# Second attention: the rotation's swapped halves brought by transfers from ScalarE's queue, not by products; query and key blocks in two banks

## The chip, the core and the metric

One core of a Trainium2 chip runs the kernel, with its engines TensorE (PE in the profile), VectorE (DVE), ScalarE (ACT), GpSimd (POOL) and SyncE (SP), the last of which only issues transfers. The metric is the time of one execution on the device in microseconds, the median of several runs.

## What is computed

The reference is a first block (a gated recurrence and a sparse attention side by side, then a feed-forward), and two further layers on the same 256 tokens of 1024 features, each an attention and a convolutional feed-forward. The change is in the attention of the first of the two further layers, called the second attention here:

```python
def apply_rope(x, cos, sin):
    half = x.shape[-1] // 2
    x1, x2 = x[..., :half], x[..., half:]
    ...
    return jnp.concatenate([x1 * c - x2 * s, x2 * c + x1 * s], axis=-1)

def moba_mixer(xn, w_qkv, w_o, cos, sin):
    ...
    q = apply_rope(qkv[:, :, 0], cos, sin)
    k = apply_rope(qkv[:, :, 1], cos, sin)
    o = moba_attention(q, k, qkv[:, :, 2])
    return o.reshape(B, S, N_HEADS_2 * HEAD_DIM) @ w_o
```

With 256 tokens there is one block, so the attention is a causal one over 16 heads of 64 features. The rotation takes each head's features in two halves of 32 and needs, beside x, the same x with its halves swapped and the second half negated.

## The kernel before

Features lie on the 128 partitions, tokens along the free dimension. All weights come from one stream of 356 chunks of 128 x 1024 numbers (512 KB), which SP loads in order into three raw buffers (L543). Every chunk is split into a high part by ScalarE (`split_high`, L1291) and a low part by VectorE (`split_low`, L1776), into rings of six, and every product of full accuracy is three products on TensorE: high with high, high with low, low with high (`split_product`, L610 to L612). The order on each engine is the order of the code; semaphores join the engines, and no scheduler decides anything.

The second attention has, after its values, 16 blocks of projections (`query_or_key`): even ones are queries, odd ones keys, each of two heads, 24 products from one chunk. Three of them come ahead, in banks 0, 1 and 2; the others all go to bank 3 and are placed by `next_queries_and_keys` between the parts of the attention, two per pair of heads j. So TensorE's order in a pair is: scores of the pair (L729), block 3 + 2j, turning of the probabilities of pair j - 2 (L741), block 4 + 2j, values of pair j - 3 (L756 to L759). The turning begins with the third pair, the values with the fourth; in the first two pairs two blocks follow each other directly.

Each block then goes through this:

- ScalarE copies it out of its bank to `rope_in` (L1637, two buffers), and goes on to the split of a chunk six ahead.
- TensorE multiplies `rope_in` by a constant matrix `rot64` of zeros, ones and minus ones into bank 7 (`turn_rope`, L1094), in the middle of the next block's products. In the trace this product is two instructions.
- VectorE (`rope`) multiplies `rope_in` by the cosines (L2216), bank 7 by the sines (L2218) and adds the two (L2219). It signals `rope_done`, for which the scores wait: pair j needs blocks 2j and 2j + 1.

ScalarE's order in a pair (`attention`, `behind_block`) is: output of pair j - 4 (L1367, from j = 4), two heads' exponentials (L1358, L1360), the copy of block 3 + 2j and a split, the copy of turned probabilities (L1374), the copy of block 4 + 2j and a split. VectorE's is: the low part of output j - 4 (L1800), two heads' row maxima (L1844, L1846), the inverse sums, block 2 + 2j, a copy of turned probabilities (L1859), block 3 + 2j. Each block on VectorE ends with a split. The code that sets where blocks go:

```python
        def qk_bank(n):
            return bank[min(n, QK_AHEAD)][:, 0:S]
...
            def rope_operand(n):
                act.wait_ge(chunk_used, BASE["qk1"] + n + 1)
                if n >= 2:
                    act.wait_ge(rope_done, n - 1)
                fn(rope_in[:, n % 2, :], qk_bank(n), ACT.Copy,
                   scale=1.0 if n % 2 else HD ** -0.5).then_inc(rope_in_ready, 1)
                split_high(BASE["qk1"] + n + RING)
```

## Time and profile before

| | |
|---|---|
| median of 3 runs | 1151.5 us (1149.93 to 1153.06) |
| the profiled execution | 1151.86 us |
| its span | 1150.1 us |
| TensorE busy | 1121.8 us, 98% |
| VectorE busy | 873.7 us, 76% |
| ScalarE busy | 689.9 us, 60% |
| chain that ended last | TensorE 82%, VectorE 7%, ScalarE 4%, transfers 3% |
| the stage of the change, first block to last scores | 572.3 to 641.1 us |

The busy time of an engine counts its arithmetic. Waiting, registers and the issuing of transfers are not in it. The start of an instruction is measured; the end of a product on TensorE is modelled, so that durations of neighbouring products overlap, and the distance of their starts is what one costs. Times of the chain and of rows count from the start of the span.

### The profile page before, as it was taken

The page shows a single profiled execution, that of the slowest core. Times are in us where ns is not written, and L with a number is a line of the kernel's source. Part 1 is how long each engine was busy: PE and PEld are TensorE (multiplying, and loading weights), DVE is VectorE, ACT ScalarE, POOL GpSimd, SP SyncE. Part 2 cuts the span into 40 slices and gives each one's busy share as a digit, 9 for nine tenths or more (in the row PEclk, how much of TensorE's full clock was granted, in tenths as well). Part 3 has the DMA queues.
Part 4 walks back from the last instruction along what each step waited for, and adds up shares of the span by engine and source line. Part 5 has one row for each costly group of instructions (what it writes and reads, how often), then busy time and mean ns, then how long its engine had stood idle before and what let it go on. Part 6 is the DMA issues. An engine that isn't in the chain of part 4 may idle for free.

```text
span 1150.1 us, 25241 instructions
## 1 busy us (share of the span) xinstructions
PE 1121.8 (98%) x9449; PEld 1086.1 (94%) x9449; DVE 873.7 (76%) x1640; ACT 689.9 (60%) x1240; POOL 89.6 (8%) x141
## 2 busy tenths in 40 slices
PE   6999999999999999999999999999999999999997
PEld 6999999988999999999899999999998889999997
DVE  5789878687587998888777578767677867877774
ACT  6757864566646666555665466555565846655554
POOL 0000000055300000000023200000001330000000
PEclk9998999999999999999999999999999999999999
DMA  6675644722274776665544247766653424776661
GB/s 224 202 217 158 201 140 130 215 80 83 62 205 142 207 225 200 192 197 185 165 147 128 82 153 223 215 193 195 187 153 121 129 76 150 225 213 196 190 195 38
DMA packets 52925, 190.89 MB, mean 166 GB/s; under 512 B 6000, under 2 KB 6256, under 8 KB 52848
## 3 DMA queue, kind: packets, MB, share of 16 engines
q1 hardware_dynamic: 52416, 188.64, 54.1%
q8 instruction: 53, 0.87, 0.3%
q10 hardware_dynamic: 432, 1.19, 0.3%
q14 instruction: 24, 0.20, 0.1%
HBM read 188.75 MB, written 1.05 MB: 165 GB/s over the span
## 4 chain that ended last, share of the span: by engine, by line
PE 82%; DVE 7%; ACT 4%; DMA 3%; issue 2%; SPq 0%; DVEq 0%; ACTq 0%
PE bank L610 24%; PE bank L611 23%; PE bank L612 23%; DMA w_raw<-weight_stream 3%; DVE w_low L1776 3%; PE bank L729 2%; PE bank L741 2%; ACT w_high L1291 1%; DVE arena L2015 1%; PE bank L618 1%; PE bank L620 1%; PE bank L619 1%; PE bank L758 1%; DVE r_low L1800 1%; PE bank L756 1%
## 5 line engine op out<-in xcount | busy, mean ns | idle before, releaser
L1776 DVE TENSOR_TENSOR w_low<-w_raw,w_high 128x1024 fp32r<-128x1024 f32 x356 | 433.8, 1223 | 137.1 <-ACT w_high L1291 134.1
L1291 ACT ACTIVATE w_high<-w_raw 128x1024 fp32r<-128x1024 f32 x356 | 374.9, 1059 | 263.3 <-PE bank L612 163.6
L610 PE MATMUL bank<-h_high,w_high 128*128 128x256 f32 x1760 | 498.4, 283 | 11.9 <-DVE h_low L1814 10.3
L611 PE MATMUL bank<-h_low,w_high 128*128 128x256 f32 x1760 | 488.8, 278 | 0.0
L612 PE MATMUL bank<-h_high,w_low 128*128 128x256 f32 x1760 | 488.7, 278 | 0.0
L610 PEld LDWEIGHTS bank<-h_high,w_high 128*128 128x128 f32 x1760 | 332.4, 189 | 17.3 <-issue 11.9
L611 PEld LDWEIGHTS bank<-h_low,w_high 128*128 128x128 f32 x1760 | 332.6, 189 | 0.4
L612 PEld LDWEIGHTS bank<-h_high,w_low 128*128 128x128 f32 x1760 | 332.3, 189 | 0.0
L610 PE MATMUL bank<-r_high,w_high 128*128 128x256 f32 x942 | 267.6, 284 | 4.7 <-ACT arena L1703 2.6
L611 PE MATMUL bank<-r_low,w_high 128*128 128x256 f32 x942 | 262.2, 278 | 0.0
L612 PE MATMUL bank<-r_high,w_low 128*128 128x256 f32 x942 | 262.2, 278 | 0.0
L610 PEld LDWEIGHTS bank<-r_high,w_high 128*128 128x128 f32 x942 | 178.4, 189 | 10.5 <-ACT arena L1703 4.7
L611 PEld LDWEIGHTS bank<-r_low,w_high 128*128 128x128 f32 x942 | 178.4, 189 | 0.3
L612 PEld LDWEIGHTS bank<-r_high,w_low 128*128 128x128 f32 x942 | 178.5, 189 | 0.0
L584 POOL TENSOR_SCALAR arena<-arena,stats 128x128 f32<-128x128 f32 (+1 forms) x128 | 82.4, 658 | 428.7 <-DVE stats L1853 428.6
L1893 DVE SCALAR_TENSOR_TENSOR arena<-arena,small 128x255 f32<-128x255 f32 (+1 forms) x184 | 87.8, 477 | 5.7 <-ACT arena L1407 2.4
L1800 DVE TENSOR_TENSOR r_low<-arena,r_high 128x256 fp32r<-128x256 f32 (+1 forms) x96 | 43.1, 450 | 7.1 <-ACT r_high L1420 4.0
L1407 ACT ACTIVATE arena<-arena,small 128x256 f32<-128x256 f32 x68 | 40.0, 588 | 13.2 <-DVE arena L1907 13.2
L1907 DVE TENSOR_TENSOR arena<-bank,rstd 128x256 f32<-128x256 f32 x68 | 28.8, 423 | 18.3 <-PE bank L612 18.2
L1358 ACT ACTIVATE arena<-bank,stats 128x128 f32<-128x128 f32 x64 | 23.3, 364 | 30.9 <-DVE stats L1846 30.9
L729 PE MATMUL bank<-arena 64*128 64x128 f32 (+3 forms) x256 | 34.4, 346 | 0.5 <-DVE arena L2295 0.3
L1420 ACT ACTIVATE r_high<-arena 128x256 fp32r<-128x256 f32 x68 | 27.8, 408 | 10.7 <-DVE arena L1931 9.6
(207 smaller groups left out, 1077.2 us busy)
## 6 DMA issues: line engine op xcount, KB each, us to landing
w_raw<-weight_stream SPq DMA_DIRECT2D x356, 512.0 KB, 4.1
x<-x_in SPq DMA_DIRECT2D x4, 256.0 KB, 6.2
small<-small_in ACTq DMA_DIRECT2D x1, 1001.5 KB, 9.1
out<-arena SPq DMA_DIRECT2D x3, 256.0 KB, 2.5
out<-arena SPq DMA_DIRECT2D x1, 128.0 KB, 2.7
out<-arena ACTq DMA_DIRECT2D x1, 128.0 KB, 2.9
small<-small_in ACTq DMA_DIRECT2D x1, 30.5 KB, 4.0
```

The lines of the kernel that those rows point to most:

```text
L584: ins = nc.gpsimd.tensor_scalar(part, part, inv_sums[:, t, h:h + 1], gate(i, t), ALU.mult, ALU.mult)
L610: mm(out_ap, wh, high, start=start, stop=False, skip_group_check=True)
L611: mm(out_ap, wh, low, start=False, stop=False, skip_group_check=True)
L612: return mm(out_ap, wl, high, start=False, stop=stop, skip_group_check=True)
L729: ins = mm(of(use.scores, i)[:, at], q(i, t)[part, :], k(i)[part, 0:P * (t + 1)], start=i not in seen, stop=i in seen, skip_group_check=True)
L1291: fn(w_high[:, c % RING, :], w_raw[:, c % RAW, :], ACT.Copy).then_inc(high_ready, 1)
L1407: fn(taps_g[:, j % 2, :], scaled_g[:, j % 2, :], ACT.Identity, scale=tap(f"fcw{n}", 2, k + j), bias=tap(f"fcb{n}", 0, k + j)).then_inc(tap ...
L1420: fn(r_high[:, j % SLOTS, :], hidden[:, j % 2, :], ACT.Copy).then_inc(hid_high, 1)
L1776: v.tensor_tensor(w_low[:, c % RING, :], w_raw[:, c % RAW, :], f(w_high[:, c % RING, :]), ALU.subtract).then_inc(low_ready, 1)
L1800: v.tensor_tensor(dst, src, f(high), ALU.subtract).then_inc(done, 1)
L1893: return v.scalar_tensor_tensor(dst[:, tokens:S], src[:, 0:S - tokens], tap(row, j), dst[:, tokens:S], ALU.mult, ALU.add)
L1907: v.tensor_tensor(scaled_g[:, slot, :], bank[slot][:, 0:S], rstd[:, :], ALU.mult).then_inc(g_scaled, 1)
```

## The change

- `qk_bank`: blocks from 3 on alternate between bank 3 (odd) and bank 7 (even). Block n waits for the copy of block n - 2, not of n - 1. Block 4 also waits until bank 7 has been read by the stage before, which the first rotation product did.
- `turn_rope`, its 16 products, the matrix `rot64` and the semaphore `rope_turned` are gone.
- ScalarE waits behind each copy for the copy's own semaphore and issues four transfers, each of 32 partitions x 256 numbers (32 KB), from `rope_in` to a new buffer `rope_swap`, so that the halves of both heads of the block are exchanged. The two buffers have a semaphore each. The split follows.
- VectorE's second product reads `rope_swap` and waits for the four transfers. The minus sign is now in the table of sines.
- The first scores also wait until their bank has been read (`rotated_and_bank`).

```diff
-         ("c64", S), ("s64", S), ("rot64", P), ("cs32", S),
+         ("c64", S), ("s64", S), ("cs32", S),
...
+        rope_swap = tiles(14336, 2)
...
-        rope_turned = sem("rope_turned")
+        rope_swapped = [sem(f"rope_halves_swapped{i}") for i in range(2)]
...
         def qk_bank(n):
-            return bank[min(n, QK_AHEAD)][:, 0:S]
+            return bank[n if n < QK_AHEAD else (QK_AHEAD, 7)[n % 2 == 0]][:, 0:S]
...
-            def turn_rope(n):
-
-                if n == 0:
-                    pe.wait_ge(acc_read, 4 * ACC_V1 + 4)
-                pe.wait_ge(rope_in_ready, n + 1)
-                if n:
-                    pe.wait_ge(rope_done, n)
-                mm(bank[7][:, 0:S], par("rot64"), rope_in[:, n % 2, :], start=True, stop=True).then_inc(rope_turned, 1)
-
             def query_or_key(n):
 
                 c = BASE["qk1"] + n
                 chunk_here(c)
-                if n > QK_AHEAD:
-                    pe.wait_ge(rope_in_ready, n)
+                if n == QK_AHEAD + 1:
+                    pe.wait_ge(acc_read, 4 * ACC_V1 + 4)
+                if n > QK_AHEAD + 1:
+                    pe.wait_ge(rope_in_ready, n - 1)
                 for k in range(DT):
                     ins = split_product(qk_bank(n), c, k * P, h_high[:, k, :], h_low[:, k, :], k == 0, k == DT - 1)
-                    if n and k == DT // 2 - 1:
-                        turn_rope(n - 1)
                 ins.then_inc(chunk_used, 1)
...
-                if (j, part) == (NH // 2 - 2, 1):
-                    turn_rope(SIZE["qk1"] - 1)
...
+            def rotated_and_bank(h):
+                pe.wait_ge(rope_done, 2 * (h // 2) + 2)
+                if h == 0:
+                    pe.wait_ge(acc_read, 4 * ACC_V1 + 3)
...
                 fn(rope_in[:, n % 2, :], qk_bank(n), ACT.Copy,
                    scale=1.0 if n % 2 else HD ** -0.5).then_inc(rope_in_ready, 1)
+                act.wait_ge(rope_in_ready, n + 1)
+                for at in range(0, P, HD // 2):
+                    other = at ^ HD // 2
+                    act.dma_start(rope_swap[at:at + HD // 2, n % 2, :], rope_in[other:other + HD // 2, n % 2, :]).then_inc(
+                        rope_swapped[n % 2], 16)
                 split_high(BASE["qk1"] + n + RING)
...
-                dve.wait_ge(rope_turned, n + 1)
-                link(v.tensor_tensor(b, bank[7][:, 0:S], s64r, ALU.mult))
+                dve.wait_ge(rope_swapped[n % 2], 64 * (n // 2 + 1))
+                link(v.tensor_tensor(b, rope_swap[:, n % 2, :], s64r, ALU.mult))
...
-    put("s64", np.sin(angles(HD)))
+    signs = np.where(row % HD < HD // 2, -1.0, 1.0).astype(np.float32)
+    put("s64", np.sin(angles(HD)) * signs[:, None])
```

ScalarE before, in the pair j = 4, behind the exponentials (L1637 is the copy, L1291 the split, L1374 the copy of turned probabilities, L1367 the next output).

```order
L1637 ACTIVATE arena<-bank3 128x256 [waits rope_done,chunk_used]
L1291 ACTIVATE w_high<-w_raw 128x1024 [waits chunk_used,chunk_loaded1]
L1374 ACTIVATE arena<-bank1 128x384 [waits pv_done,probs_turned]
L1637 ACTIVATE arena<-bank3 128x256 [waits rope_done,chunk_used]
L1291 ACTIVATE w_high<-w_raw 128x1024 [waits chunk_used,chunk_loaded2]
L1367 ACTIVATE r_high<-bank2 128x256 [waits pv_done]
```

The same place after the change (the copy is now L1632, the transfers L1637, the split L1286, the copy of turned probabilities L1369, the output L1362):

```order
L1632 ACTIVATE arena<-bank3 128x256 [waits rope_done,chunk_used]
L1637 DMA arena<-arena 32x256 [waits rope_operand_ready]
L1637 DMA arena<-arena 32x256 x3
L1286 ACTIVATE w_high<-w_raw 128x1024 [waits chunk_used,chunk_loaded1]
L1369 ACTIVATE arena<-bank1 128x384 [waits pv_done,probs_turned]
L1632 ACTIVATE arena<-bank7 128x256 [waits rope_done,chunk_used]
L1637 DMA arena<-arena 32x256 [waits rope_operand_ready]
L1637 DMA arena<-arena 32x256 x3
L1286 ACTIVATE w_high<-w_raw 128x1024 [waits chunk_used,chunk_loaded2]
L1362 ACTIVATE r_high<-bank2 128x256 [waits pv_done]
```

Eight transfers stand between copies and splits, and the second block is read from bank 7.

TensorE before, at the turn from one pair to the next (the end of a block of pair j = 1, the scores of pair 2, and the head of its first block up to the rotation product; left out are the products L611 and L612 and the L610 that only repeat):

```order
L1094 MATMUL bank7<-arena,small 128x256 [waits rope_done,rope_operand_ready]
L610 MATMUL bank3<-h_high,w_high 128x256
L729 MATMUL bank4<-arena 128x128 [waits rope_done,probs_ready]
L729 MATMUL bank5<-arena 128x256 [waits rope_done]
L729 MATMUL bank4<-arena 128x256
L729 MATMUL bank5<-arena 128x128
L610 MATMUL bank3<-h_high,w_high 128x256 [waits rope_operand_ready,low_ready]
```

The same place after the change:

```order
L611 MATMUL bank7<-h_high,w_high 128x256
L730 MATMUL bank4<-arena 128x128 [waits rope_done,probs_ready]
L730 MATMUL bank5<-arena 128x256 [waits rope_done]
L730 MATMUL bank4<-arena 128x256
L730 MATMUL bank5<-arena 128x128
L611 MATMUL bank3<-h_high,w_high 128x256 [waits rope_operand_ready,low_ready]
```

The rotation product is gone, and the scores still wait for `rope_done`.

## Rows read from the trace of the kernel before

**Rows 1.** The page: busy time of TensorE, and granted clock in 40 slices.
```profile
PE 1121.8 (98%) x9449; PEld 1086.1 (94%) x9449; DVE 873.7 (76%) x1640; ACT 689.9 (60%) x1240; POOL 89.6 (8%) x141
...
PEclk9998999999999999999999999999999999999999
```

**Rows 2.** Busy times by stretch, cut at starts of scores; then the stages behind.
```profile
core 0: us, PE busy (x) PEld busy (x) DVE busy (x) ACT busy (x) POOL busy (x), PEclk, DMA share, GB/s
581.34:589.65 8.31, 7.73 (x61) 7.17 (x60) 5.98 (x17) 5.55 (x13) 0.00 (x0) 1.00 0.59 183
...
615.27:624.36 9.09, 9.09 (x78) 8.34 (x76) 6.98 (x19) 5.03 (x15) 2.93 (x4) 1.00 0.41 116
...
633.46:641.10 7.64, 7.64 (x64) 6.95 (x62) 6.61 (x19) 4.34 (x13) 2.93 (x4) 1.00 0.39 112
657.00:1110.00 453.00, 445.99 (x3812) 437.23 (x3812) 342.53 (x583) 259.68 (x439) 24.36 (x36) 1.00 0.58 175
```

**Rows 3.** Timeline of TensorE around the first rotation product (start us, us, instruction).
```profile
576.02 0.28 PE L611 MATMUL bank<-h_low,w_high 128*128 128x256 f32 x1
576.14 0.28 PE L612 MATMUL bank<-h_high,w_low 128*128 128x256 f32 x1
576.25 0.59 PE L1094 MATMUL bank<-arena,small 128*128 128x256 f32 x2
576.50 0.47 PE L610 MATMUL bank<-h_high,w_high 128*128 128x256 f32 x1
576.80 0.28 PE L611 MATMUL bank<-h_low,w_high 128*128 128x256 f32 x1
```

**Rows 4.** Timeline of TensorE from block 3 to block 4.
```profile
585.37 0.28 PE L612 MATMUL bank<-h_high,w_low 128*128 128x256 f32 x1
586.23 0.36 PE L610 MATMUL bank<-h_high,w_high 128*128 128x256 f32 x1 [0.58 <-ACT arena L1637]
```

**Rows 5.** Timeline of ScalarE: copies of blocks 0 and 1.
```profile
575.60 0.40 ACT L1637 ACTIVATE arena<-bank 128x256 f32<-128x256 f32 x1
...
578.27 0.39 ACT L1637 ACTIVATE arena<-bank 128x256 f32<-128x256 f32 x1 [1.29 <-PE bank L612]
```

**Rows 6.** Timeline of ScalarE in the pair j = 4, in brackets what it waited.
```profile
615.79 0.38 ACT L1367 ACTIVATE r_high<-bank 128x256 fp32r<-128x256 f32 x1
617.30 0.37 ACT L1358 ACTIVATE arena<-bank,stats 128x128 f32<-128x128 f32 x1 [1.14 <-DVE stats L1846]
...
619.62 0.38 ACT L1637 ACTIVATE arena<-bank 128x256 f32<-128x256 f32 x1 [0.61 <-PE bank L612]
...
623.66 0.38 ACT L1637 ACTIVATE arena<-bank 128x256 f32<-128x256 f32 x1 [2.32 <-PE bank L612]
623.94 1.05 ACT L1291 ACTIVATE w_high<-w_raw 128x1024 fp32r<-128x1024 f32 x1
624.88 0.38 ACT L1367 ACTIVATE r_high<-bank 128x256 fp32r<-128x256 f32 x1
```

**Rows 7.** Timeline of VectorE: second product and sum of block 11.
```profile
622.27 0.42 DVE L2218 TENSOR_TENSOR arena<-bank,arena 128x256 f32<-128x256 f32 x1 [1.05 <-PE bank L1094]
622.73 0.43 DVE L2219 TENSOR_TENSOR arena<-arena 128x256 f32<-128x256 f32 x1
```

**Rows 8.** Transfers: issues on both queues, median landings by line, rate near the end.
```profile
1.19 1.85 SPq L549 DMA_DIRECT2D x<-x_in  x4
...
4.74 0.33 ACTq L1437 DMA_DIRECT2D small<-small_in  x1
...
w_raw<-weight_stream SPq DMA_DIRECT2D x356, 512.0 KB, 4.1
...
out<-arena SPq DMA_DIRECT2D x3, 256.0 KB, 2.5
...
out<-arena ACTq DMA_DIRECT2D x1, 128.0 KB, 2.9
...
1146.00:1148.00 2.00, 0.00 (x0) 0.00 (x0) 0.78 (x3) 0.00 (x0) 0.00 (x0) 0.50 1.02 368
```

More of the change, by code:

```diff
@@ L1148, in _ @@
                       lambda h, t: v1[:, t, h * HD:(h + 1) * HD], probs1, probs_t1, LATER_BANKS,
-                      lambda h: pe.wait_ge(rope_done, 2 * (h // 2) + 2), next_queries_and_keys)
+                      rotated_and_bank, next_queries_and_keys)
             for k in range(3, DT - LATE):
@@ L2467, in lay_out_small @@
     put("cs32", turned)
-    rot = np.zeros((P, P))
-    for at in range(0, P, HD):
-        for j in range(HD // 2):
-            rot[at + HD // 2 + j, at + j] = -1.0
-            rot[at + j, at + HD // 2 + j] = 1.0
-    put("rot64", rot)
     norms = [a["norm1_g"], a["norm2_g"], a["norm_mix_2"][0], a["norm_ffn_2"][0], a["norm_mix_2"][1],
```

## The prediction

> **What bounds the kernel now.** I read the page first [rows 1]: TensorE is busy for 1121.8 of 1150.1 us, while VectorE has 76% and ScalarE 60%. Work taken from TensorE is therefore worth its full time, provided nobody else becomes late. Then I cut the second attention into its eight pairs of heads, one stretch from the start of one pair's scores to the start of the next, and asked for busy times by stretch [rows 2]. The reader is to see three things there. There are three stretches of 8.3 us (the row of the first stands there; TensorE idles 0.58 of its 8.31), three of 9.1 and one of 7.64, so the seven run from 581.34 to 641.10. TensorE is full in the later ones. ScalarE shows only 4.3 to 5.6 us of work, but that counts neither waits nor the issuing of transfers. Behind the stage TensorE stays 98% busy (445.99 of 453.00 us, the last of [rows 2]), so a shift of 641.10 is carried to the end nearly whole.
>
> **What goes from TensorE.** One rotation product per block, 16 in all. Around the first, the start of an ordinary product is 0.66 us after that of the one ahead of it, with two more products (this one, and its successor) between; undisturbed, two steps are 0.23 [rows 3]. So each costs 0.43 us, and 16 cost 6.9. Two stand before 581.34, two in each stretch. The second bank also ends a wait: block 4 started 0.86 us behind the last product of block 3 in place of 0.12 [rows 4], because ScalarE had not emptied the one bank. That is 0.74 us, twice (the other blocks have turns or scores between them): 1.5. Gross gain 8.4 us. TensorE's own need falls to 6.7, 6.7, 7.4, three times 8.25 and 6.78 us. No stretch can be shorter.
>
> **What comes on ScalarE.** Behind each copy it waits for that copy's end and issues four transfers before its next weight split. The price of an issue (I below) is bounded by ScalarE's own one in mid-flow, 0.33 us, and by four in a row on SP's queue, 1.85 us, or 0.46 each with the gaps between [rows 8]. I take 0.37: the row of the same engine, and a little for the gaps. Four are 1.48 us per block, 23.7 us in all, of a kind the busy columns don't show. Also the split used to start 0.28 us behind the copy's start [rows 6]; now the copy (0.38) and its semaphore (some 0.09, an estimate) come first, 0.47.
>
> **What comes on the path of a block.** From issue to landing (L) no row shows a transfer inside the local memory. Above it stand the last store, 128 KB in 2.9 us, and a weight load, 512 KB under load, 4.1; below it the 256 KB stores with 2.5, less 0.7 for moving 256 KB at the 368 GB/s of that stretch, so 1.8 [rows 8]. I take 2.2: a swap moves 32 KB a piece, but the weight stream has 0.39 to 0.59 of the engines in this stage [rows 2]. All four must have landed, and the fourth starts 3I behind the first.
>
> At this place the Trainium skill speaks against counting I at all: DMA: Bandwidth & Descriptors, "Issuing engines are not separate DMA queues", says that the issuing sequencer's time is usually small beside the transfer. The rows say 4I = 1.48 against L = 2.2, which is not small; what the rule would give is the second rival.
>
> **The sum.** *First scores.* ScalarE copies block 0 at 575.60 [rows 5] as before; + 0.47 + 1.48, + 0.95 for the split (623.94 to 624.88 is its step [rows 6]) = 578.50, a little behind the end of block 1's product, since that copy used to start at 578.27. Then copy 0.47, three more issues 1.11, landing 2.2, VectorE's second product and the sum, which were 0.46 + 0.43 [rows 7], with 0.05 to be seen by TensorE: 0.94. The scores start at 583.2, not 581.34.
>
> *Stretches 1 to 4.* The scores of the next pair need the block that this pair's first projection yields. Its copy started 4.35 us behind the scores (615.27 to 619.62, [rows 2, 6]), 3.92 without the rotation product. From there 0.47 + 3I + L + 0.94: a stretch is 5.33 + 3I + L = 8.64 us. TensorE needs 6.7 to 8.25, so it waits in all four.
>
> *Stretches 5 to 7.* From the fifth pair on ScalarE also writes the first attention outputs. Its loop was 615.79 to 624.88 = 9.09 us, in which it waited 0.61 and 2.32 for TensorE [rows 6]. These it can give up, but not the 1.14 for VectorE, which must first take the low part of that output and then the row maxima. That leaves 6.16. Two blocks add 2 x (4I + 0.19) = 3.34: 9.50 us, where TensorE needs 8.25, 8.25 and 6.78.
>
> So the last scores start at 583.2 + 4 x 8.64 + 3 x 9.50 = 646.3, where they started at 641.10: **5.2 us later**. In short, the end is at 630.4 + 43 I for L = 2.2. The product's 8.4 us are gained, and 13.6 us of new waits on TensorE take their place. Edits at nothing: the 64 KB less in the constants are loaded in the first microseconds behind other loads; VectorE's product reads SBUF in place of a bank, and takes 0.42 us either way ([rows 7] has one from a bank and a sum from SBUF, 0.42 and 0.43); the weight splits of these blocks come later on both engines, but serve products six chunks ahead, two or three stretches of cover; SP's queue is passed by nothing, only its stream shares the engines. What is queued behind ScalarE's issues is counted: the split, the copy of turned probabilities (for products a stretch later), the next block's copy. VectorE waits in place for the swap, and its low split and the next row maxima stand behind it; it used to begin the second product 2.65 us behind ScalarE's copy (619.62 to 622.27, of which 1.05 waiting [rows 6, 7]) and would now at 0.47 + 1.11 + 2.2 = 3.78, which is the same delay as the scores', seen from the other side.
>
> The profiled execution took 1151.86 us at a span of 1150.1; the median is 1151.5. Against either, + 5.2: 1156.7 on the median.
>
> **Bounds.** With I = 0.33 and L = 1.8: first scores at 582.5, then 3 x 8.12, 8.25 and 3 x 9.18: 642.7, + 1.6. With I = 0.46 and L = 2.9: 584.6, 4 x 9.61, 3 x 10.22: 653.7, + 12.5.
>
> **Rivals.**
> 1. *Slower, much: the swap queues behind the weights.* If each lands like a weight load (4.1 us, [rows 8]), a stretch is 5.33 + 1.11 + 4.1 = 10.5 us in all seven, the first scores start at 585.1, and the last at 658.9: + 17.8, 1169.3 us. For it: the stream's share of 0.6 in the first stretches. Against: 32 KB are a sixteenth of a load, and the share falls to 0.4. The same page of the Trainium skill, "Rules for kernel authors", says that pieces on disjoint partitions don't run beside each other and advises one transfer; if the four add up rather than overlap, this is the result. Chance 0.07.
> 2. *The other side: issuing does not hold ScalarE.* If the issues run beside its arithmetic (I near 0), the first scores start at 577.84 + 0.47 + 2.2 + 0.94 = 581.4, three stretches take 7.53, three take TensorE's 8.25, the last 7.53: 636.3, 4.8 us earlier, 1146.7 us. It decides below I = 0.25, where 630.4 + 43 I passes 641.1. For it: the profile counts issuing as no work of the engine, so the sequencer might run ahead. Against: the issues stand between a finished copy and the next split, in order. Chance 0.11, with a little between.
> 3. *TensorE's clock.* The forecast leaves it 2.7 us idle in a stretch. For it: the granted clock is lower in the fourth slice of the page [rows 1], so it can fall inside this program. Against: it was 1.00 in the stretch with 0.58 us of idleness, and in the 453 us that hold 7 [rows 2]. Eight microseconds at 1.2 for 2.4 GHz would add 4 to the forecast: 1160.7. Chance 0.05.
> 4. *Nothing changes in what is done.* The instruction lists show the products gone and 64 issues there, so I give this none.
>
> **Chances.** Forecast 0.77, with + 1.6 to + 12.5; three tenths of that, small I and quick landing, are under 3.45 us, 0.3% and about what a measurement can tell. Together: faster 0.10, within 0.3% 0.24, slower 0.66. The range leaves out the second rival and the first, and reaches from just under no change, 1150.5, to + 11.5, 1163.0.
>
> **What would show it.** 64 issues of 0.33 to 0.46 us on ScalarE's queue, 16 x 4 landings near 2.2; score starts 8.6 us apart four times, then 9.5 three times; TensorE waiting for VectorE's sum before each scores, 0.4 to 2.7 us; ScalarE no longer waiting for TensorE in stretches 5 to 7. Wrong would be: issues under 0.25, stretches of 7.5 to 8.3, or clock rows under 1.00.

## The result, and the profile after

The changed kernel takes 1185.8 us (median of 4 runs, 1182.6 to 1186.1), where the kernel before took 1152.3 beside it (4 runs): a ratio of 1.0287, interval 1.0261 to 1.0312. The direction was forecast, the size was not: + 33.5 us, where + 5.2 was expected and the range ended at + 11.5. The profiled execution took 1182.63 us.

Page of the changed kernel: busy times, granted clock in 40 slices, chain, queue and transfers. They answer to [rows 1] and to the landings of [rows 8]. In the last two lines the number behind KB is the median time to landing.

```profile
PE 1128.1 (96%) x9417; PEld 1093.1 (93%) x9417; DVE 872.5 (74%) x1640; ACT 690.6 (58%) x1240; POOL 88.6 (8%) x141
...
PEclk9998999999999999999978999999999999999999
...
PE 76%; DVE 9%; ACT 6%; DMA 5%; issue 2%; ACTq 2%; SPq 0%; DVEq 0%
...
w_raw<-weight_stream SPq DMA_DIRECT2D x356, 512.0 KB, 4.3
arena<-arena ACTq DMA_DIRECT2D x64, 32.0 KB, 1.9
```

TensorE has 32 matmul records fewer, the 16 rotation products of two instructions each, and yet it is busy for 6.3 us longer. That can't be work. The clock row says what it is: 0.7 and 0.8 in the 21st and 22nd slice, which lie in the changed stage, where [rows 1] had 9 in both.

The changed kernel by stretches between starts of scores (columns as in [rows 2]):

```profile
586.37:599.41 13.04, 9.19 (x57) 8.70 (x57) 6.09 (x17) 5.77 (x13) 0.00 (x0) 0.76 0.46 140
599.41:611.47 12.06, 9.60 (x57) 9.10 (x57) 6.03 (x18) 4.49 (x12) 3.21 (x4) 0.74 0.36 103
611.47:622.17 10.70, 8.86 (x62) 8.54 (x63) 6.41 (x19) 4.75 (x13) 1.71 (x4) 0.84 0.39 109
622.17:634.87 12.70, 9.64 (x71) 8.97 (x71) 6.49 (x19) 4.76 (x13) 1.71 (x4) 0.87 0.42 122
634.87:646.34 11.47, 9.65 (x70) 9.09 (x71) 6.81 (x20) 5.14 (x14) 3.21 (x4) 0.85 0.38 111
646.34:658.45 12.11, 9.63 (x71) 8.89 (x71) 6.82 (x20) 5.14 (x14) 3.38 (x4) 0.86 0.38 109
658.45:670.63 12.18, 6.93 (x58) 6.16 (x59) 6.80 (x20) 5.03 (x14) 3.37 (x4) 1.00 0.37 107
```

The first scores start at 586.37 (forecast 583.2, before 581.34), the last at 670.63 (646.3, 641.10). So 29.5 of the profiled execution's 30.8 us lie ahead of the last scores. Of these, 1.2 arose ahead of the stage: ScalarE copies block 0 at 576.76 here and at 575.60 in [rows 5]; over all runs below this start lies between 573.6 and 578.1. No stretch is near the 8.64 or 9.50 us of the forecast, and the clock is under 1.00 in six of seven. ScalarE's arithmetic is 4.5 to 5.8 us in 12; what fills its time is in no busy column.

The transfers' line of the changed kernel, with durations of one issue in nanoseconds (least, median, most) and times to landing:

```profile
L1637 ACTq DMA_DIRECT2D arena<-arena x64: 514/612/1571, 577.2 to 666.1; - x64
...
DMA to landing us min/median/max: 1.8/1.9/4.9
```

An issue holds ScalarE's queue for 0.61 us, nearly twice the 0.33 of the same engine's issue in [rows 8]. Waits of the changed kernel from 572 to 700 us (total, times, longest):

```profile
DVE arena L2218 <- DMA arena<-arena: 34.9, 12, 4.7
ACT w_high L1286 <- issue: 32.7, 12, 3.5
PE bank L730 <- DVE arena L2219: 24.3, 8, 4.7
```

All eight scores wait, for 24.3 us together, where none waited before. Timeline around the second scores, ScalarE (copy L1632, split L1286), its queue, SP's queue and VectorE (second product L2218; the sum L2219 starts 0.46 us behind it):

```profile
592.87 0.38 ACT L1632 ACTIVATE arena<-bank 128x256 f32<-128x256 f32 x1 [0.62 <-PE bank L613]
593.29 2.46 ACTq L1637 DMA_DIRECT2D arena<-arena  x4
...
593.50 0.33 SPq L544 DMA_DIRECT2D w_raw<-weight_stream  x1
595.85 1.06 ACT L1286 ACTIVATE w_high<-w_raw 128x1024 fp32r<-128x1024 f32 x1 [2.59 <-PE bank L613]
...
598.38 0.43 DVE L2218 TENSOR_TENSOR arena<-arena 128x256 f32<-128x256 f32 x1 [4.66 <-DMA arena<-arena]
...
599.41 1.65 PE L730 MATMUL bank<-arena 64*128 64x128 f32 x8 [3.85 <-DVE arena L2219]
```

The copy ends at 593.25, four issues take 2.46 us, and VectorE has its operand only at 598.38. During the first of these issues SP issues a weight load of 512 KB. The scores then take 1.65 us at half clock; at full clock they take 0.92. From the chain of the changed kernel, the step from the fourth issue to its landing (start, us):

```profile
583.55 1.85 DMA arena<-arena
595.13 3.22 DMA arena<-arena
608.54 1.86 DMA arena<-arena
619.22 1.90 DMA arena<-arena
629.89 3.92 DMA arena<-arena
642.61 2.68 DMA arena<-arena
```

There are two kinds, 1.9 us and 2.7 to 3.9. Those starting at 595.13 and 629.89 have a fresh weight load beside them (SP's queue has issues at 593.50 and 629.75), and 642.61 one issued 2.2 us ahead (640.39). The trace's 64 transfers bear this out: the 25 that are issued between 0.4 us ahead of a weight load's issue and 2.3 us behind it land after 3.3 us in the median, the other 39 after 1.9.

So three things are to be told apart: ScalarE's time in issues, late landings, and the clock.

### The profile page after: what moved, and what is told of

Its sections match the earlier page's. It is cut to its first block, busy times and chain, and to the rows that moved or that the text cites. A ratio compares the mean times of both kernels' runs of the same rounds, so it can differ in the third digit from the quotient of the medians.

```text
span 1180.8 us, 25226 instructions
## 1 busy us (share of the span) xinstructions
PE 1128.1 (96%) x9417; PEld 1093.1 (93%) x9417; DVE 872.5 (74%) x1640; ACT 690.6 (58%) x1240; POOL 88.6 (8%) x141
## 4 chain that ended last, share of the span: by engine, by line
PE 76%; DVE 9%; ACT 6%; DMA 5%; issue 2%; ACTq 2%; SPq 0%; DVEq 0%
PE bank L611 23%; PE bank L612 22%; PE bank L613 22%; DMA w_raw<-weight_stream 3%; DVE w_low L1776 3%; PE bank L730 2%; ACTq L1637 2%; DMA arena<-arena 2%; ACT w_high L1286 2%; PE bank L742 1%; DVE arena L2015 1%; PE bank L619 1%; PE bank L621 1%; PE bank L620 1%; DVE r_low L1800 1%
## 5 line engine op out<-in xcount | busy, mean ns | idle before, releaser
L1286 ACT ACTIVATE w_high<-w_raw 128x1024 fp32r<-128x1024 f32 x356 | 374.9, 1059 | 304.5 <-PE bank L613 178.9
L611 PE MATMUL bank<-h_high,w_high 128*128 128x256 f32 x1760 | 500.6, 284 | 10.3 <-DVE h_low L1814 10.3
L612 PE MATMUL bank<-h_low,w_high 128*128 128x256 f32 x1760 | 493.5, 280 | 0.0
L611 PEld LDWEIGHTS bank<-h_high,w_high 128*128 128x128 f32 x1760 | 337.4, 192 | 14.7 <-issue 11.0
L612 PEld LDWEIGHTS bank<-h_low,w_high 128*128 128x128 f32 x1760 | 337.2, 192 | 0.0
L613 PEld LDWEIGHTS bank<-h_high,w_low 128*128 128x128 f32 x1760 | 337.1, 192 | 0.0
L611 PE MATMUL bank<-r_high,w_high 128*128 128x256 f32 x942 | 267.9, 284 | 7.3 <-ACT arena L1703 2.5
L612 PE MATMUL bank<-r_low,w_high 128*128 128x256 f32 x942 | 262.5, 279 | 0.0
L611 PEld LDWEIGHTS bank<-r_high,w_high 128*128 128x128 f32 x942 | 178.7, 190 | 13.6 <-ACT arena L1703 4.7
L612 PEld LDWEIGHTS bank<-r_low,w_high 128*128 128x128 f32 x942 | 178.4, 189 | 0.3
L730 PE MATMUL bank<-arena 64*128 64x128 f32 (+3 forms) x256 | 37.3, 372 | 24.8 <-DVE arena L2219 24.3
L730 PEld LDWEIGHTS bank<-arena 64*128 64x128 f32 (+1 forms) x256 | 28.2, 202 | 31.3 <-issue 24.5
```

What stands on the lines that cost most here:

```text
L611: mm(out_ap, wh, high, start=start, stop=False, skip_group_check=True)
L612: mm(out_ap, wh, low, start=False, stop=False, skip_group_check=True)
L613: return mm(out_ap, wl, high, start=False, stop=stop, skip_group_check=True)
L730: ins = mm(of(use.scores, i)[:, at], q(i, t)[part, :], k(i)[part, 0:P * (t + 1)], start=i not in seen, stop=i in seen, skip_group_check=True)
L1286: fn(w_high[:, c % RING, :], w_raw[:, c % RAW, :], ACT.Copy).then_inc(high_ready, 1)
```

## The experiments

"Beside it" is the kernel before in the same group of runs: 1153.1 us for the first four experiments, 1150.9 for the next four, 1151.1 for the four behind those, 1151.6 for the last. A difference between medians of two groups therefore carries up to 2 us of drift.

**1. No exchange at all.** Neither transfers nor products; VectorE's second product reads `rope_in`, so the exchange of the halves is left out.

```diff
-                for at in range(0, P, HD // 2):
-                    other = at ^ HD // 2
-                    act.dma_start(rope_swap[...], rope_in[...]).then_inc(rope_swapped[n % 2], 16)
...
-                dve.wait_ge(rope_swapped[n % 2], 64 * (n // 2 + 1))
-                link(v.tensor_tensor(b, rope_swap[:, n % 2, :], s64r, ALU.mult))
+                link(v.tensor_tensor(b, rope_in[:, n % 2, :], s64r, ALU.mult))
```

> The changed kernel without any swap: no transfers and no rotation products, VectorE multiplies the unswapped copy by the sines (so the rotation is left out). Issue theory (each of the 64 issues holds ScalarE and the block's path for 0.61 us), landing theory (the swap collides with weight loads) and clock theory (TensorE's waits let its clock fall) all expect what the products cost before: 1152.3 - 8.4, about 1144 us, clock rows of 1.00 in the stage, and no wait of the scores over 1 us. If instead something else in the change costs the 33 us (the second bank, the new table of sines), this kernel stays above 1152.

Measured 1143.7 us (1142.8 to 1144.4), ratio 0.9915 (0.9898 to 0.9931), - 9.4 us. Two stretches of it:

```profile
580.46:586.96 6.50, 6.50 (x56) 6.23 (x56) 6.29 (x17) 5.32 (x13) 0.00 (x0) 1.00 0.58 183
608.60:616.67 8.07, 8.07 (x72) 7.54 (x70) 6.80 (x19) 5.04 (x15) 3.64 (x4) 1.00 0.39 128
```

TensorE is full in both. The forecast's gross gain of 8.4 us holds within 1 us. Its bounds for TensorE, 6.7 and 8.25 us, which no stretch was to undercut, are 0.2 too high. All of the 42 us between this kernel and the changed one are the price of the transfers and of what they set off.

**2. The other half alone: two banks, products kept.** Blocks alternate between banks 3 and 7, and from block 3 on each block's rotation product goes to the second half of its own block's bank, while the next block fills the other bank.

```diff
-            return bank[min(n, QK_AHEAD)][:, 0:S]
+            return bank[n if n < QK_AHEAD else (QK_AHEAD, 7)[n % 2 == 0]][:, 0:S]
+
+        def turned_rope(n):
+            return bank[QK_AHEAD if n > QK_AHEAD - 1 and n % 2 else 7][:, S:2 * S]
...
-                mm(bank[7][:, 0:S], par("rot64"), rope_in[:, n % 2, :], start=True, stop=True).then_inc(rope_turned, 1)
+                mm(turned_rope(n), par("rot64"), rope_in[:, n % 2, :], start=True, stop=True).then_inc(rope_turned, 1)
...
-                    pe.wait_ge(rope_in_ready, n)
+                    pe.wait_ge(rope_done, n - 1)
```

> The kernel before with one part of the change alone: blocks in two banks, rotation by products as before (into the second half of banks 3 and 7). All theories expect the two bank waits of 0.74 us to go and a little to come from waiting for the sum of block n - 2: 0 to 1.5 us less than before, 1150.8 to 1152.3. More than 1153 would say that the second bank itself costs.

Measured 1150.7 us (10 runs, 1149.5 to 1152.7), ratio 0.9978 (0.9968 to 0.9987), - 2.4 us. Its first stretch:

```profile
583.87:591.28 7.41, 7.41 (x61) 7.03 (x61) 5.96 (x17) 5.56 (x13) 0.00 (x0) 1.00 0.55 174
```

It took 8.31 before; the wait of 0.58 us of [rows 4] is gone. From the copy of block 0 (578.12) to the last scores (641.33) it is 63.2 us, where it was 65.5 (575.60 to 641.10), so the gain lies in the stage. It is more than the 0 to 1.5 us expected: stretches 3 to 6, where no wait was counted, are shorter by 0.2 each. This version is faster than the kernel before by 0.2%.

**3. Transfers with one bank.** The changed kernel with all later blocks in bank 3.

```diff
-            return bank[n if n < QK_AHEAD else (QK_AHEAD, 7)[n % 2 == 0]][:, 0:S]
+            return bank[min(n, QK_AHEAD)][:, 0:S]
```

> The changed kernel with the other part undone: transfers as they are, all later blocks in bank 3 again. Issue and landing theory: TensorE waits for VectorE before every scores anyway, so a bank wait of some 0.5 us in front of a block is partly hidden: within 1185 to 1190. Clock theory: the waits are cut into more pieces, and the clock rows may differ either way, within 1180 to 1192.

Measured 1183.3 us (1181.3 to 1186.2), ratio 1.0265 (1.0242 to 1.0288). Beside the transfers the second bank is worth nothing: TensorE waits longer for other things.

**4. The clock: filler products.** 16 products that nobody reads, ahead of each scores and into their own bank, so that TensorE works through its wait. 128 products more than the changed kernel.

```diff
+                        for _ in range(16):
+                            mm(of(use.scores, 2 * j)[:, 0:S], h_high[:, 0, 0:P], h_high[:, 1, :], start=True, stop=True, ...)
```

> The changed kernel with 16 more products of 128 x 256 ahead of each of the eight scores, where TensorE waits 1.8 to 4.7 us, into a bank that the scores then overwrite: 128 products, 14.6 us of work at full clock. Clock theory: they keep the granted clock at 1.00 through the stage, and the time falls by 6 to 14 us, to 1172 to 1180, although work is added. Issue and landing theory without the clock: no change, 1184 to 1188, or up to 5 us slower where a wait is shorter than the filler. A slower time with clock rows still at 0.5 to 0.8 leaves the clock theory open.

Measured 1175.8 us (1173.8 to 1179.6), ratio 1.0202 (1.0176 to 1.0228): 128 products more, 10 us less. Its sixth stretch:

```profile
640.96:652.40 11.44, 10.16 (x86) 9.43 (x86) 6.80 (x20) 5.03 (x14) 3.38 (x4) 1.00 0.37 116
```

The clock is 1.00 from 592 us on (in the first stretch it is still 0.78), and the stretches from the second on are still 10.2 to 11.4. The clock is a part, not the whole.

**5. Issues without the wait.** All 64 are issued; VectorE reads `rope_in` and waits for none (the exchange is left out). ScalarE waits for the swap of two blocks before, and VectorE once for all of them behind the stage.

```diff
                 if n >= 2:
                     act.wait_ge(rope_done, n - 1)
+                    act.wait_ge(rope_swapped[n % 2], 64 * (n // 2))
...
-                link(v.tensor_tensor(b, rope_swap[:, n % 2, :], s64r, ALU.mult))
+                link(v.tensor_tensor(b, rope_in[:, n % 2, :], s64r, ALU.mult))
```

> All 64 transfers are issued as in the changed kernel, but VectorE's second product reads rope_in and waits for none of them (ScalarE waits for the swap of two blocks before, which has long landed; the rotation's exchange is left out). It holds the price of issuing alone. If issuing holds ScalarE for 0.61 us each (2.5 us a block, as the trace of the changed kernel has it), its loop in the last stretches is 6.16 + 2 x (2.5 + 0.19) = 11.5 us, the earlier ones 8.3 to 10: 1165 to 1172 us, so most of the loss stays. If the landing is what costs (rival: L, and its collisions with the weight loads), this kernel is close to the one without any transfers, 1144 to 1149 us.

Measured 1171.0 us (1170.4 to 1172.6), ratio 1.0180 (1.0163 to 1.0197). That is 27 of the 42 us over experiment 1 with no landing on VectorE's path (29 if each is taken against the kernel before beside it). ScalarE in one stretch of it:

```profile
630.34 0.40 ACT L1633 ACTIVATE arena<-bank 128x256 f32<-128x256 f32 x1
630.77 2.44 ACTq L1638 DMA_DIRECT2D arena<-arena  x4
633.31 1.06 ACT L1286 ACTIVATE w_high<-w_raw 128x1024 fp32r<-128x1024 f32 x1 [2.57 <-issue]
634.27 0.47 ACT L1369 ACTIVATE arena<-bank 128x384 f32<-128x384 f32 x1
634.65 0.38 ACT L1633 ACTIVATE arena<-bank 128x256 f32<-128x256 f32 x1
```

Nothing between two rows is a wait for another engine. The copies of the same place come 11.32 us apart, three times running (619.02, 630.34, 641.66, 652.98). In that time ScalarE waits once, 1.14 us for VectorE's row maxima, as in [rows 6]; otherwise it is full, with 2 x 2.54 us in issues, which the page counts as idle.

**6 and 7. One transfer per block.** Experiment 6: 128 partitions unswapped, 128 KB. Experiment 7: only the first of the four, 32 KB. The exchange is left out in the one, three quarters of it in the other.

```diff
-                for at in range(0, P, HD // 2):
+                for at in (0,):
...
-                dve.wait_ge(rope_swapped[n % 2], 64 * (n // 2 + 1))
+                dve.wait_ge(rope_swapped[n % 2], 16 * (n // 2 + 1))
```

> One transfer per block in place of four: all 128 partitions, unswapped, 128 KB as before (the rotation's exchange is left out). VectorE waits for it as in the changed kernel. If the count of issues sets the price: 0.6 us per block on ScalarE instead of 2.5, no stretch is above TensorE's own need plus the landing by more than a few tenths, 1146 to 1153 us. If bytes or landings set it (rival), 128 KB in one piece takes as long as four of 32 KB in a row, and the time stays at 1175 us or above.

> One transfer per block of 32 partitions, 32 KB (the other three pieces are left out, so most of the exchange is). If only the count of issues matters, the same as the one transfer of 128 KB within 1.5 us. If the length of one transfer matters too, it is faster than that by 16 x the difference of the landings, 2 us or more.

Measured 1153.6 us (10 runs, 1147.6 to 1161.9) and 1153.5 (10 runs, 1150.8 to 1159.8); ratios 1.0029 (1.0004 to 1.0054) and 1.0021 (1.0009 to 1.0034). The same median for four times the bytes: their number in a transfer does not show here, the number of transfers does. Experiment 6 lies 0.6 us above the 1146 to 1153 expected, and both have a wide spread, to which experiment 11 comes back.

**8. SP issues the swaps**, between its weight loads (its loop is written out for this stage); ScalarE issues nothing.

```diff
+            def swap(n):
+                sp.wait_ge(rope_in_ready, n + 1)
+                for at in range(0, P, HD // 2):
+                    other = at ^ HD // 2
+                    sp.dma_start(rope_swap[...], rope_in[...]).then_inc(rope_swapped[n % 2], 16)
...
+                if 0 <= n < SIZE["qk1"] - 1:
+                    swap(n + 1)
+                load(c)
```

> The same four swaps per block, issued by SP between its weight loads; ScalarE does not wait for its copy and issues nothing. If it is ScalarE's time that counts (3 x 0.61 + L on the path, but no stretch bound by ScalarE's loop): stretches of 5.33 + 1.83 + 1.9 = 9.1 us in all seven, first scores near 583.5, last near 647: + 6, 1158 us, and 1158 to 1166 with the clock falling behind waits of 1 to 2 us. If the loss is in the path of one block (issues in a row, landing, and the collisions, which are more when swaps and loads share a queue), it stays at 1172 us or above.

Measured 1170.4 us (1168.7 to 1170.7), ratio 1.0164 (1.0147 to 1.0181), over the 1158 to 1166 expected and under the 1172 of the rival. Its median landing was 2.5 us. Two of its stretches, 9.09 and 9.05 us long, are the 9.1 of the path; the other five are 10.3 to 11.1. One of each:

```profile
606.27:617.08 10.81, 8.70 (x63) 8.22 (x63) 6.66 (x19) 4.76 (x13) 3.09 (x4) 0.85 0.42 117
626.17:635.22 9.05, 8.04 (x70) 7.47 (x71) 7.05 (x20) 5.03 (x14) 1.87 (x4) 1.00 0.53 150
```

Taking the issues off ScalarE helps. What lengthens the five is not late landings: on the chain only the first landing is long (3.53 us, ahead of the first scores), the other seven take 1.80 to 1.89. Four of the five have a clock of 0.80 to 0.85, and the fifth has one issue of 1.85 us. So in a kernel whose path is 9.1 us, a lower clock goes with 1.6 to 2.0 us more per stretch.

**9. Loads held back.** The changed kernel, with SP issuing a weight load of this stage only when the swap at hand has landed.

```diff
+            def swap(n):
+                sp.wait_ge(rope_swapped[n % 2], 64 * (n // 2 + 1))
...
+                if 0 <= n < SIZE["qk1"] - 1:
+                    swap(n + 1)
+                load(c)
```

> The changed kernel with one more wait: in this stage SP issues the weight load of a chunk only when the swap of the block then at hand has landed, so a load never starts in the middle of a swap. In the changed kernel the fourth landings on the chain that ran against a fresh load took 3.2 to 3.9 us in place of 1.9, in four stretches of eight. If these collisions cost 5 to 8 us, this kernel takes 1177 to 1182 us and its landings stay under 2.3. If the long landings are no collisions with a fresh load but the stream as a whole, or if they fall beside other waits, it stays within 2 us of the changed kernel (1185.8), or gets slower by late weights.

Measured 1178.7 us (1174.7 to 1181.2), ratio 1.0231 (1.0205 to 1.0258): 7 us less, by a wait more. The landings on its chain:

```profile
582.92 1.85 DMA arena<-arena
594.38 1.91 DMA arena<-arena
605.05 1.86 DMA arena<-arena
...
660.00 1.91 DMA arena<-arena
```

None of the long ones is left on the chain. So the long landings had cost the 7 us, as far as the held loads change nothing else. The second half of the expectation fell, though: over all 64 the median rose from 1.9 to 2.3 us, and the longest is 3.8. The held loads now run beside the other block's swap, whose lateness costs less.

**10 and 11. Fillers again**, with issues alone (as 5) and with one transfer of 128 KB (as 6); the edit is that of 4.

> Issues alone (as in the run of 1171.0) with 16 filler products before each scores, as in the run with fillers. Without the waits for the landing that kernel's granted clock still fell (0.8 to 0.9 in three slices). If a low clock is part of its 27 us over the kernel without transfers, the fillers give 5 to 10 us back: 1161 to 1167, and what stays, about 20 us, is ScalarE's time in issues. If it is ScalarE's time alone, the fillers change nothing or cost up to 3 us: 1170 to 1174.

> One unswapped transfer per block (the run with 1147.6 to 1161.9, a wide spread) with the 16 fillers before each scores. If the spread and the 10 us over the kernel without transfers come from TensorE's clock, its runs lie close together, near 1148 to 1151 and not above 1153. If they come from landings of 2.0 to 4.7 us, the spread stays and the median stays at 1153 or rises by the fillers' own time.

Measured 1173.6 us (1172.5 to 1174.8), ratio 1.0194 (1.0177 to 1.0211), and 1161.2 us (1159.9 to 1162.2), ratio 1.0085 (1.0069 to 1.0102). With issues alone the fillers give nothing, although they keep the clock at 1.00 up to the last stretch: ScalarE sets the pace there, and a faster TensorE waits longer. Four of the seven stretches agree with those of experiment 5 within 0.1 us (10.5, 9.4, 10.2 and 11.3). Two stretches of experiment 10 are 13.2 and 14.7 us long, and the same two are 12.7 each in experiment 5; why was not followed up. In experiment 11 the spread shrinks from 14 us (10 runs) to 2 (4 runs), as the clock theory had it, but the median is above the 1153 it allowed. I had taken the fillers for free. They are not where TensorE is full:

```profile
593.52:601.94 8.42, 8.42 (x73) 8.14 (x73) 6.14 (x17) 4.62 (x13) 3.37 (x4) 1.00 0.49 157
```

8.42 against the 6.50 of experiment 1 is 0.12 us for each of the 16. Less 128 x 0.12 = 15.4 us, experiment 11 would be at 1146, two above experiment 1 (four, if each is taken against the kernel before beside it). The wide spread of experiments 6 and 7 thus comes with the clock: the fastest run of experiment 6, 1147.6, has a mean granted clock of 0.995, the slowest, 1161.9, one of 0.985. That the 10 us over experiment 1 are all clock is not shown. In the profiled execution of experiment 6 the first landing on the chain takes 4.75 us, and four later ones 2.6 to 3.2, so late landings have a part.

**12. Two transfers of 64 partitions**, unswapped (the exchange is left out).

> Two unswapped transfers of 64 partitions per block (the exchange is left out): between the one (1153.6) and the four (1185.8). With 0.6 us per issue and 2 x the issues per pair on ScalarE's loop, 6.16 + 2 x (1.2 + 0.19) = 8.9 us in the last stretches, 5.33 + 0.6 + 1.9 = 7.8 in the first: 1152 to 1160 us. If the time grows in proportion to the count, it is 1153.6 + 10.7 = 1164; above 1168 would mean that the first additional issue costs more than the others.

Measured 1170.9 us (1167.5 to 1172.3), ratio 1.0163 (1.0146 to 1.0180): above the 1152 to 1160 expected, above the 1164 of a time in proportion to the count, and above the 1168 that was to mean that the first additional issue costs more than the others. From one transfer to two it is 17 us, from two to four 15. The windows and the chain of its stretch from 627.41 show another bound:

```profile
627.41:637.71 10.30, 8.05 (x71) 7.48 (x71) 6.72 (x20) 5.57 (x16) 3.38 (x4) 1.00 0.46 129
```

```profile
631.72 0.47 ACTq L1636
632.22 4.43 DMA arena<-arena
...
642.11 0.47 ACTq L1636
642.61 4.74 DMA arena<-arena
```

The clock is full, ScalarE waits 1.69 us for the row maxima ahead of its exponentials, and the second transfer takes 4.4 to 4.7 us to land, as long as a weight load. The path formula 5.33 + I + L with 0.5 and 4.4 gives 10.2, which is this stretch. Here rival 1 of the prediction is what happens. The landings ahead of the eight scores take 4.03, 2.04, 4.03, 2.26, 4.07, 4.43, 4.74 and 3.06 us, so it happens in five of eight. In four of these five SP issues a weight load from 0.1 us ahead of the second transfer's issue to 0.2 us behind it; ahead of the first scores the load comes 1.9 us behind.

**13. Fillers and held loads together.** What was open: issues of 0.61 us with their gaps give + 18 us, the kernel shows + 33.5. The expectation below calls these 18 us the forecast's own formulas. They are not quite: those give + 15, since they have 9.1 us for each of stretches 1 to 4, and the 9.9 comes from ScalarE's loop as the changed kernel shows it.

> The changed kernel with both: 16 filler products before each scores, and SP's weight loads held back until the swap at hand has landed. With issues of 0.61 us and gaps of 0.03, the forecast's own formulas give first scores at 584.8, four stretches of 9.9 (ScalarE's loop, no longer the path of 9.1) and three of 11.6: last scores at 659.2, which is + 18 us, 1169 to 1171. If clock (10 us regained by fillers) and collisions (7 us regained by held loads) are two separate costs, this kernel takes 1185.8 - 17 = 1169, the same. If they are one cost seen twice (a collision makes TensorE wait, and the wait lets the clock fall), it stays at the time with fillers alone, 1174 to 1177.

Measured 1171.4 us (1170.5 to 1177.2; three of the four under 1171.6), ratio 1.0190 (1.0162 to 1.0217). Its stretches:

```profile
586.09:596.25 10.16, 8.50 (x72) 8.14 (x72) 5.95 (x17) 5.67 (x13) 0.00 (x0) 1.00 0.40 123
596.25:605.63 9.38, 8.69 (x72) 8.34 (x72) 6.24 (x18) 4.28 (x12) 1.71 (x4) 1.00 0.47 142
...
615.39:625.49 10.10, 10.10 (x86) 9.44 (x86) 6.52 (x19) 4.66 (x13) 1.71 (x4) 1.00 0.45 135
625.49:636.51 11.02, 10.16 (x88) 9.44 (x87) 6.69 (x20) 5.04 (x14) 3.38 (x4) 1.00 0.39 118
636.51:647.79 11.28, 10.16 (x86) 9.43 (x86) 6.80 (x20) 5.04 (x14) 3.38 (x4) 1.00 0.41 117
647.79:659.15 11.36, 9.04 (x74) 8.11 (x74) 6.81 (x20) 5.04 (x14) 3.37 (x4) 1.00 0.39 117
```

Four stretches of 9.85 on the mean and three of 11.22, where 9.9 and 11.6 were expected, and the last scores at 659.15, expected 659.2. That the end agrees to 0.1 us is in part luck: the first scores are 1.3 us late, 0.6 of it from ahead of the stage, and in one stretch TensorE is full with the fillers (10.10 of 10.10). The gains, 10 and 7 us singly, are 14.4 together: mostly two costs, not one seen twice. With the clock at full and the long landings off the scores' way, what is left over the kernel before is 19.8 us: issues, undisturbed landings and what the fillers cost, less the product's gain.

## Why the forecast was wrong

**What held.** The product's price and the wait that the second bank ends: 8.4 us gross, 9.4 measured. From a copy's start to its first issue, where the 0.09 us in the forecast's 0.47 rested on no row: 0.42 measured (592.87 to 593.29). What follows behind the stage: 1.2 us of the 30.8 came there. The mechanism: ScalarE's issues and the landing delay VectorE's sum, and TensorE waits for it. In the last three stretches ScalarE waits for TensorE only once ahead of a copy, 1.30 us in the fifth; its 1.14 us for the row maxima stay. The median landing, 1.9 us, lies in the bounds of L and under the 2.2 taken.

**The step that failed: the price I of an issue.** "I take 0.37", between 0.33 and 0.46, was read from issues of other transfers, from memory off the core. These, inside the local memory, take 0.61 us, and 0.03 lies between two. The formula end = 630.4 + 43 I was the place to see the danger: each tenth in I is 4.3 us. In the forecast's steps with I = 0.635 and L = 1.9, and with ScalarE's loop for stretches 1 to 4 (worked out from the rows above):

| | forecast | its steps and ScalarE's loop, I and L measured | experiment 13 | changed kernel |
|---|---|---|---|---|
| first scores | 583.2 | 584.8 | 586.09 | 586.37 |
| a stretch of 1 to 4 | 8.64 | 9.9 | 9.4 to 10.2 | 10.7 to 13.0 |
| a stretch of 5 to 7 | 9.50 | 11.6 | 11.0 to 11.4 | 11.5 to 12.2 |
| last scores | 646.3 | 659.3 | 659.15 | 670.63 |

The 9.9 is another loop than the forecast's: at 0.37 the path of a block bounds the early stretches, at 0.61 that path is only 9.1 and ScalarE's loop of two copies, two splits, four exponentials and eight issues is longer (in the changed kernel from 615.08 to 625.48, less 0.5 us in which it waited). At 0.37 the same loop would be 7.8, so the forecast was right to leave it out. The forecast's own formulas, with I and L as measured, end at 656.2, and this loop adds 3.1. So 13 of the 24.3 us by which the last scores missed the forecast are the one price, carried by two loops; with it alone the sum is + 15 to + 18, and outside the range. The other 11 are late landings, the clock, and the 1.2 us from ahead of the stage. The bounds were no bounds: rows of another kind of transfer can't exclude a dearer one, and above 0.46 nothing in the profile spoke against anything.

**The step behind it: L as one number.** L is 1.9 us or up to 3.9, by whether a weight load has just been issued. The prediction had rival 1 for this, as all or nothing, with 0.07. The four pieces of a block do not add up: from 597.21 on they are issued 0.6 us apart with no weight load issued within 1.5 us of any, and each lands 1.8 to 1.9 us behind its own issue. But lateness beside a load is real in some stretches of the changed kernel, 7 us by experiment 9, and in five of eight landings of experiment 12.

**Rival 3, the clock.** It had 0.05 and 4 us. The argument against it was that the clock stayed at 1.00 with 0.58 us idle in a stretch [rows 2]. That speaks of idleness of 0.58 us and not of 1.8 to 4.7 in one piece, as the changed kernel has it. Windows of the changed kernel behind the first, second, fourth and sixth scores:

```profile
588.00:592.00 4.00, 4.00 (x21) 4.00 (x20) 2.30 (x11) 3.81 (x9) 0.00 (x0) 0.50 0.54 171
...
599.41:604.00 4.59, 4.59 (x22) 4.27 (x23) 3.90 (x14) 2.77 (x9) 1.44 (x2) 0.50 0.44 129
...
622.80:626.10 3.30, 3.30 (x18) 3.08 (x15) 2.08 (x11) 1.58 (x4) 1.30 (x4) 0.50 0.57 149
646.70:650.00 3.30, 3.30 (x18) 2.98 (x16) 1.67 (x7) 1.33 (x2) 0.00 (x0) 0.50 0.53 143
```

Behind waits of 4.70 and 3.85 us it is 0.50, the lower of its two levels, 1.2 GHz. Behind waits of 1.84 (ahead of 622.17) and 1.81 us (ahead of 646.34) it is 0.50 too, and behind one of 2.48 (ahead of 658.45) it stays 1.00. So waits no longer than the forecast's own 2.7 us can lower the clock, and 0.05 was too little for this rival. The fillers are worth 10 us. The Trainium skill, TensorE: Matmul & The Clock Gate, "HAM oscillation — how this bites in real kernels", describes such a case, a wait for a transfer behind which the next products start slow. The trace agrees, with 1.65 us for scores that take 0.92.

**Rival 2, free issuing, is excluded** by experiment 5: issues that nobody on VectorE waits for cost 27 us. The rule of the Trainium skill that stood beside it (DMA: Bandwidth & Descriptors, "Issuing engines are not separate DMA queues": an issuer's time is usually small beside the transfer) does not fit this trace, where one issue takes 0.61 us beside a landing of 1.9, and the four of a block 2.44.

**The account** of the 42 us over experiment 1: about 28 for the issues and undisturbed landings (experiment 13), of which fillers on a full TensorE may be a part; 14 for clock and long landings, 10 and 7 if mended singly. How much of the 28 is landing was not measured by itself.

## What to carry to other kernels

Price an issue by a row of the same kind of transfer, and where there is none, put its price as an unknown into the formula and ask at what value the change turns: here break-even was 0.25 us an issue, under every row. A chain of small transfers between a producer and a consumer that are both busy costs its issuer by the number of transfers, not by their bytes, and its lateness twice: once as TensorE's wait, and again as a lower clock behind it. A copy that must be there in the next few microseconds should not start beside a 512 KB load; holding the load back can be the cheaper wait.

## What the runs showed of the hardware

- An issue from local memory to local memory on ScalarE's queue, alone or as the first of a block, takes 0.51 us at 32 partitions (experiment 7 and the changed kernel) and 0.47 at 64 and 128 (experiments 12 and 6); one directly behind another takes 0.61, at 32 partitions and at 64. SP's queue has 0.59 in the median for the same transfers (experiment 8). A load of the constants takes 0.33 [rows 8]. One transfer of 128 KB and one of 32 KB land alike, 2.5 and 2.2 us in the median.
- Of the 64 landings of the changed kernel 33 take 1.8 to 2.0 us and 23 take 2.6 to 4.9, mostly those with a weight load issued just before or behind them.
- Of the changed kernel's eight waits of TensorE ahead of scores, 1.8 to 4.7 us long, seven were followed by the lower clock; one of 2.5 us was not.
- Products added to a kernel made it 10 us faster, since TensorE had work in its waits.
- A wait added on SP made the kernel 7 us faster.
